# Indexer heads of a sparse-attention layer issued in pairs, their products alternating between two 32-row strips of TensorE

## The reference, cut to what matters

```python
def dsa_attend(q, qi, wi, pos_q, k, v, ki, pos_k, topk):
    rel = relu(einsum('bthd,bsd->bths', qi, ki))          # 8 indexer heads, width 32
    score = einsum('bths,bth->bts', rel, wi) * (IDX_DIM ** -0.5 * N_IDX_HEADS ** -0.5)
    score = where(admissible[None], score, -inf)           # chunk-causal
    top_val, top_idx = top_k(score, topk)
    ...
    p = softmax(logits of the selected keys)
    o = einsum('btkgs,btskd->btkgd', p, v_sel)
```

## Time and profile before

| | us |
|---|---|
| median of 3 runs | 1511.53 |
| lowest, highest | 1510.69, 1512.97 |
| span of the profiled execution | 1508.3 |
| difference of the median and that span | 3.2 |
| PE busy | 1483.1 |
| DVE, ACT, POOL busy | 664.4, 521.8, 185.1 |

### The profile page before, as it was taken

How to read it: one execution, slowest core, us unless ns; L and a number is a source line. 1 busy time by engine, 2 the same in 40 slices (tenths; PEclk the granted TensorE clock), 3 DMA queues, 4 the chain that set the end, 5 groups by cost and what they waited for, 6 DMA issues and landing times.

```text
span 1508.3 us, 22280 instructions
## 1 busy us (share of the span) xinstructions
PE 1483.1 (98%) x9329; PEld 1323.6 (88%) x9329; DVE 664.4 (44%) x1172; ACT 521.8 (35%) x956; POOL 185.1 (12%) x215
## 2 busy tenths in 40 slices
PE   6999999999999999999999999999999999999997
PEld 5766766899999999999976677669999999999997
DVE  5257632245444444444623683213454444344453
ACT  5365542233213223133335553323332231321322
POOL 4246200020000000000214540000100000000011
PEclk8999755799999999999999995559999999999998
DMA  6211200033232222222321120001322222222221
GB/s 180 70 57 43 74 5 0 0 85 85 85 84 78 82 80 85 84 84 83 104 82 45 40 78 25 5 1 42 85 75 82 83 84 84 85 85 85 82 59 63
DMA packets 169252, 102.37 MB, mean 68 GB/s; under 512 B 6920, under 2 KB 159424, under 8 KB 169152
## 3 DMA queue, kind: packets, MB, share of 16 engines
q1 hardware_dynamic: 169152, 100.94, 23.0%
HBM read 96.98 MB, written 3.95 MB: 67 GB/s over the span
## 4 chain that ended last, share of the span: by engine, by line
PE 97%; DVE 1%; DMA 1%; ACT 1%; issue 0%; SPq 0%; DVEq 0%; ACTq 0%
PE bank L1334 61%; PE bank L1108 15%; PE bank L1219 6%; PE bank L1255 4%; PE bank L1235 3%; PE bank L1126 2%; PE bank L1270 2%; PE bank L1286 1%; PE bank L1140 1%; DMA late<-in_x_prompt 1%; PE bank L1200 1%; PE bank L1353 0%; PE bank L1069 0%; PE bank L1085 0%; ACT L677 0%
## 5 line engine op out<-in xcount | busy, mean ns | idle before, releaser
L521 ACT ACTIVATE ring_hi<-ring_raw 128x1024 fp32r<-128x1024 f32 x176 | 184.8, 1050 | 305.4 <-PE bank L1334 248.6
L1334 PE MATMUL bank<-vh,ring_hi 128*128 128x288 f32 x1280 | 275.4, 296 | 0.0
L1334 PE MATMUL bank<-vl,ring_hi 128*128 128x288 f32 x1280 | 275.2, 296 | 0.0
L1334 PE MATMUL bank<-vh,ring_lo 128*128 128x288 f32 x1280 | 275.2, 296 | 0.0
L766 DVE TENSOR_TENSOR ring_lo<-ring_raw,ring_hi 128x1024 fp32r<-128x1024 f32 x164 | 213.6, 1302 | 132.5 <-ACT ring_hi L521 125.5
L1334 PE MATMUL bank<-xh,ring_hi 128*128 128x288 f32 x1024 | 220.8, 297 | 0.0
L1334 PE MATMUL bank<-xl,ring_hi 128*128 128x288 f32 x1024 | 220.2, 296 | 0.0
L1334 PE MATMUL bank<-xh,ring_lo 128*128 128x288 f32 x1024 | 220.2, 296 | 0.0
L1334 PEld LDWEIGHTS bank<-vh,ring_hi 128*128 128x128 f32 x1280 | 205.2, 189 | 0.0
L1334 PEld LDWEIGHTS bank<-vh,ring_lo 128*128 128x128 f32 x1280 | 205.2, 188 | 0.0
L1334 PEld LDWEIGHTS bank<-vl,ring_hi 128*128 128x128 f32 x1280 | 205.2, 189 | 0.0
(11 more groups left out here) (161 smaller groups left out, 1608.9 us busy)
## 6 DMA issues: line engine op xcount, KB each, us to landing
ring_raw<-in_w_ff SPq DMA_DIRECT2D x128, 512.0 KB, 4.1
ring_raw<-in_w_in SPq DMA_DIRECT2D x32, 512.0 KB, 3.7
ring_raw<-in_w_out SPq DMA_DIRECT2D x16, 512.0 KB, 4.2
late<-in_x_prompt SPq DMA_DIRECT2D x4, 512.0 KB, 5.7
out_y_prompt<-late SPq DMA_DIRECT2D x4, 512.0 KB, 2.9
w_sp<-in_w_spatial SPq DMA_DIRECT2D x2, 512.0 KB, 4.2
gate_bc<-in_gate_norm SPq DMA_DIRECT2D x2, 256.0 KB, 4.9
out_k_prompt<-z SPq DMA_DIRECT2D x2, 256.0 KB, 4.3
```

The source lines that it names most:

```text
L521: s.activation(ring_hi[:, n % NSLOT, :], ring_raw[:, n % NRAW, :], ACT.Copy).then_inc(hi_ready, 1)
L1334: last = mm(bank[2 * (u % 4) + half][:, 0:HALF], w[:, k, :], a[:, k, HALVES[half]], start=k == order[0] and w is wh and a is ah, stop=k == ...
```

## The change

`INDEX_AT` puts i = 16 to 31 in pairs too, at g = 39, 41, ..., 53: half as many groups are followed by heads, each by two. `index_pair(i)` issues heads i and i + 1 together: for each of the three products first head i's, then head i + 1's. The pair's first product waits for the relu of head i - 1, so both banks are empty; there is one wait to a pair where there was one to a head. Each head still raises `idx_done` with its own last product. ACT, POOL and DVE keep their code; what is dealt out by `INDEX_AT` moves with it.

```diff
-        INDEX_AT = [FIRST_TR + 5 + (i // 2 if i < 2 * NIH else i - 2 * NIH // 2) for i in range(NX)]
+
+        INDEX_AT = [FIRST_TR + 5 + (i // 2 if i < 2 * NIH else i // 2 * 2 - 2 * NIH // 2) for i in range(NX)]
...
-                def index(i):
-                    t, hh = INDEX[i]
+                def index_pair(i):
+                    t, rows = INDEX[i][0], ROWS[INDEX[i][0]]
...
-                    if i >= 2:
-
-                        pe.wait_ge(idx_relu, NX * l + i - 1)
-                    b, rows = 32 * (hh % 4), ROWS[t]
+                    if i:
+
+                        pe.wait_ge(idx_relu, NX * l + i)
                     kh, kl = (kish, kisl) if t == SMP else (kih, kil)
                     for a, k in ((qih, kh), (qih, kl), (qil, kh)):
-                        last = mm(bank[5 + i % 2][0:rows, 0:KEYS[t]], a[b:b + ID, hh // 4, cols(t)], k[b:b + ID, 0:KEYS[t]],
-                                  start=a is qih and k is kh, stop=a is qil)
-                    last.then_inc(idx_done, 1)
+                        for m in (i, i + 1):
+                            hh = INDEX[m][1]
+                            b = 32 * (hh % 4)
+                            last = mm(bank[5 + m % 2][0:rows, 0:KEYS[t]], a[b:b + ID, hh // 4, cols(t)], k[b:b + ID, 0:KEYS[t]],
+                                      start=a is qih and k is kh, stop=a is qil)
+                            if a is qil:
+                                last.then_inc(idx_done, 1)
...
-                            else:
-                                index(i)
+                            elif i % 2 == 0:
+                                index_pair(i)
```

## The result

| | before | after |
|---|---|---|
| first measurement, median of 4 runs, us | 1512.25 | 1434.22 |
| lowest, highest | 1510.69, 1517.67 | 1423.30, 1499.54 |
| span of the profiled execution | 1508.3 | 1421.4 |
| all runs of this study but one | 60 runs, median 1511.8 | 16 runs, median 1486.0, from 1422.3 to 1506.2 |

The change is faster: the ratio is 0.946 with a 95% interval from 0.939 to 0.953, in which the 1499.54 us run is left out. By the medians of all runs, 1486.0 and 1511.8, the ratio is 0.983. The forecast of 1496.2 us, 1491.0 to 1501.5, missed it; of the 16 runs only two lie in it. Two runs, one of 4650.9 us of the kernel before and one of 1972.9 us of a variant, are left out everywhere.

A forecast was written before the change was run, and what follows sets the result against it. PE, busy 98% of the span, was taken to bound the kernel. 7.8 us a layer from pairing, less 0.1 for DVE and 0.05 for waits, gave 15.3 us over both layers: 1496.2 us, range 1491.0 to 1501.5.

The forecast's parts named there:

- The pace, and the cost of a single head and of a pair: Projection stretch on PE: products every 0.2325 us; a pair costs what a single head does; 7.8 us saved a layer.
- The order within a pair is worth 0: Heads i = 0 to 15: alternating their products gains 0, at most 0.01 us for each of eight pairs.
- The wait costs 0: PE's pair waiting for the relu of head i - 1: 1.2 us spare, cost 0, at most 0.02 a pair.
- DVE: DVE's list up to `gv_norm`: 1.4 us longer, gating products slip 0.5 us; 0.1 us a layer, bounds 0 to 0.6.
- The sum: Both layers' projection gain less the DVE and wait costs: 2 x (7.8 - 0.1 - 0.05) = 15.3 us saved.
- The clock: Attention stages: an earlier start may turn either stage's clock, 5.7 us up or down; no change taken for the sum.
- The case: Attention stages: one turns slow, +5.7 us, 1502 to 1503, or the opposite way, 1490.5; chance 0.14 with a turned stage.

The follow-up runs named there:

- the clock out of the way: Changed kernel and kernel before, each with two filler products ahead of each attention head of tiles 0, 1 and the sample: medians 1423.46 and 1438.50 us.

## Why the prediction missed

*The pace, and the cost of a single head and of a pair.* Right: 0.92 and 1.09 us a head, 1.09 us a pair of tile 3, the stretch shorter by 7.86 us (7.8 worked out), rows as forecast.

*The order within a pair is worth 0.* Right: 0.01 us a pair in the traces, nothing in the totals. The Trainium skill, page "TensorE: Matmul & The Clock Gate", section "The mechanism", says that products start in the order of issue. For products in different strips the rows refute it: the old order in the new places gives rows "x2" of 0.45 us as well.

*The wait costs 0.* Nearly right: ACT ended 1.1 us of PE's idle time before the heads in three places of the whole execution, 0.7 in two before, so 0.4 us more where 0.1 had been taken.

*DVE.* Its run from the tile 3 step to `gv_norm` was forecast at 33.8 us and is 126.28 to 160.09, 33.8. The gating products slipped by 0.9 us, not 0.5. `gv_norm` came 1.54 us later against PE, not 1.3. The timeline of PE at the start of the stage, the answer to the earlier trace rows:

```profile
160.99 1.97 PE L1274 MATMUL bank<-late,w_spT 128*128 128x64 f32 x16 [0.82 <-DVE late L896]
162.89 0.48 PE L1223 MATMUL bank<-late 64*128 64x128 f32 x2
163.30 0.33 PE L1239 MATMUL bank<-ident,att 128*128 128x128 f32 x1
```

The wait for the exponential covered all but 0.25 us of it (3.85 us from the stage's first product to the first transpose, 3.60 before); 0.1 had been taken, 0 to 0.6 as bounds. One reading was wrong: the table of places was charged with the 1.4 us, but undoing it made DVE later in the trace. Two tiles worked by turns take 2.24 us for four steps, one by itself 1.52 for two, and the prediction left out the four steps of tile 2 that no longer stand alone ahead of the wait.

*The sum.* 15.3 us forecast, 14.7 to 15.4 measured with the clock out of the way.

*The clock.* Here it failed, at the sentence "I take no change for the sum and keep it for the range", with 5.7 us as the most that a stage could turn. That bound was the difference of two stages of one execution. Both happened to be of the long kinds, and I took them for the two ends. The stages then shrank by 36.7 and 38.2 us. The work bounds it otherwise: at a clock of 0.5 PE was busy 78.50 of 78.50 us, so a stage that is nearly all at the lower level could shrink toward half; the shortest seen, 76.65 us, is 59% of 129.93. Stages of 76.65 to 134 us exist. The range would have had to reach down to 1420. How likely a turn of that size was, the rows before couldn't tell: the three runs had none, and 4 of 60 and 7 of 16 were counted afterwards. The case was named among the rivals, priced six times too small.

The size of the miss is partly luck: the first four runs had three with short stages. Six later runs of the same changed kernel had a median of 1486.0 us, and six more one of 1500.8, which lies in the forecast range without making the step on the clock any better.

## What to carry to other kernels

Small products slipped between large ones cost mostly entering and leaving (0.40 of 0.92 us here); put them side by side in different row strips and banks, and the second is free, in whatever order they are issued. Before forecasting a change of a few microseconds, look for a stage in which TensorE is fully busy at the lower clock: here it took from 77 to 132 us in one and the same kernel, and a comparison of two kernels must count such jumps over many runs, or hold the clock, before it says what the change did. A stage like that is also the largest gain in sight: 24 cheap filler products a layer, none in tile 1 and two ahead of each of the sample's heads, took 75 us off the changed kernel's median of 16 runs, though two of six runs still lost the clock once (1438 and 1440 us).

## What the runs showed of the hardware

The granted clock of one and the same stage takes, in the kernels without fillers in it, one of several courses, drawn anew in each execution and each layer: down to the end or nearly (127 to 132 us), back for 6.8 us only (123 to 128), back to stay (87 to 92), never down (76.65). At the lower level PE showed no idle time at all for 78.5 us and the clock stayed down, while at the upper one it held with PE idle 1.66 of 54.52 us.

The Trainium skill, page "TensorE: Matmul & The Clock Gate", section "A second HAM failure mode: psum-queue depth-cycling", describes short idles between groups of products that make the clock swing. The traces agree that it swings inside such a stage, and added dense products held it up in many runs: 28 of 41 with 24 to 48 of them a layer, two ahead of each of the sample's heads, but none of six with 24 laid one ahead of each head. That the idles are the cause is not shown: no kernel closed them alone, and the four products ahead of the first transpose left the 0.8 us before the gating products open.

Products of two heads in different 32-row strips start within 0.03 us of each other, and the later head's first product starts before the earlier head's second, whichever was issued first.
